# Where a gate's chunks of cached values stand in TensorE's order: between its halves, or all behind it

## The chip, the cores and the metric

One core of one Trainium2 chip runs the whole program. The metric is device time in microseconds (us) of one launch. Three runs of the kernel before gave 1912.76, 1916.53 and 1919.4 us; their median, 1916.53 us, is the time before. The profile was taken in a further execution of 1910.06 us.

## What is computed

Two decoder layers over 256 prompt tokens and 32 sample tokens (8 sequences of 4). Each layer projects the normed rows, mixes them by a pooling branch and by attention over three head groups, gates both branches, and adds a feed-forward part (dense in the first layer, experts in the second). The part around the change is the attention of the sample tokens over the caches, and the gates. Cut to that:

```python
u, q, k, v, gates = project(rmsnorm(xs, norm_attn[layer]), w_in[layer], ...)
for gi, (win, dil) in enumerate(ATT_GROUPS):        # (128,1), (512,4), (2048,16)
    c = caches[gi][layer]                            # keys c[:, :, 0], values c[:, :, 1]
    o, l = band_attention_sample(q[:, :, gi], k_all, v_all, n_past, dil, win // dil, slopes[gi])
...
g = sigmoid(gates)
h = g[..., 0, :] * (pool_o @ w_bp) + g[..., 1, :] * (att_o @ w_ba)
x = x + h @ w_o
```

All products with weights are done to float32 accuracy.

## The kernel before, in words

**Chunks.** Everything large comes from HBM in chunks of 1 MB, all issued by SyncE (SP) in one fixed order into a ring of five slots (RING, L54). Chunk c goes into the slot of chunk c-5, and SP waits in `send` (L819) until that one is done with: a weight chunk when VectorE (DVE) has made its low part (semaphore `lo_ready`), a cache chunk when TensorE (PE) has used it (`raw_used`). As SP waits in order, a chunk that can't be issued yet holds up all that stand behind it.

**Weights.** A weight chunk is split in two before PE uses it: `split_high` (L1544, ScalarE, ACT) and then `split_low` (L1824, DVE), into one of two split buffers. PE waits for the low part in `chunk` (L980). A tile of 128 output columns is 24 matmuls of 128x288.

**The stage of the change**, once per layer, stands between the scores over the cached keys and the branch tiles. On PE it has two kinds of work. Eight gates, G0 to G7, each one weight chunk of `w_in`, in two halves a and b of 24 matmuls (`gates`, L1272). And eighteen chunks of cached values, V0 to V17, four tiles each (`cache_values`, L1255): no split, PE multiplies the loaded chunk itself, with 32 columns of probabilities as weights. V0 and V9 open the sums of the first and the second four sequences and begin with three more matmuls for the new tokens. Behind G0b PE turns the probabilities of the second half (`turn_s_probs`), behind G4b it gathers the heads of the first four sequences (`gather_heads`, L1247), behind G7b those of the second. The order of both kinds is a table, `V_BEHIND` (L110): how many value chunks stand behind each half of each gate. `value_steps` (L113) makes PE's order of it (walked at L1278), `value_loads` (L127) makes SP's order.

A slot is told free late by a little: `release` (L1166) puts the signal on a list, and PE's next matmul that carries no signal of its own takes it along (`signal`, L944). The slot of a value chunk comes free when the first matmul behind the chunk is through.

**SP's order of the stage** is G0 V0 G1 V1 V2 G2 V3 V4 V5 G3 V6 V7 G4 V8 V9 V10 G5 V11 V12 G6 V13 V14 G7 V15 V16 V17, and then B0 to B3 (the branch weights, two loads of 512 KB each) and the four chunks of `w_out`. By the rule of five slots V3 takes the slot of V0, G3 that of V2, G4 that of V4, G5 that of V7, G6 that of V9, V13 that of V10, V17 that of V13, and B0 that of V14.

**The end of the stage.** DVE's list runs, for G7: the low part of B0 (`split_low`), then G7a's scaling, `own_columns(1)` (L2061) on the finished sum of the cached values, then G7b's scaling. PE's `gather_heads(1)` needs `own_columns(1)`, and so stands behind the splitting of B0. The branch tiles follow.

```python
for kind, n, x in V_STEPS:                 # L1278, PE
    if kind == "V":
        cache_values(n)
        continue
    gates(n, x)
```

Of the kernel before, what the change touches and what calls it, by code (L numbers as in the profile page):

```python
# [106 lines left out]
    return a.astype(np.float32), m.astype(np.float32), spread.astype(np.float32)  # L107


V_BEHIND = ((1, 1), (1, 1), (2, 1), (1, 1), (2, 1), (1, 1), (1, 1), (2, 0))  # L110


def value_steps():  # L113

    out, v = [], 0
    for gate, behind in enumerate(V_BEHIND):
        for x, n in enumerate(behind):
# [2452 lines left out]
```

How the kernel before makes its waits and increments, by code:

```python
            def wait_free(self, e, job):  # L706
                b, u = self.where[job]
                e.wait_ge(free[b], self.base(b) + u + 1)
# [1 line left out]
            def wait_full(self, e, job):  # L710
                b, u = self.where[job]
                e.wait_ge(full[b], self.base(b) + u + 1)
# [1 line left out]
            def wait_read(self, e, job):  # L714
                b, u = self.where[job]
                e.wait_ge(free[b], self.base(b) + u + 2)
# [1 line left out]
            def wait_before(self, e, bank):  # L719
                e.wait_ge(free[bank], self.base(bank) + self.start[bank] + 1)
# [26 lines left out]
        def wait_chunk(e, L, c):  # L748
            e.wait_ge(loaded[c % RING], 16 * (L * dmas_until(N_LAYER, c % RING) + dmas_until(c + 1, c % RING)))
# [1 line left out]
        def wait_expert_chunk(e, seq, c):  # L751
            e.wait_ge(expert_loaded[c % E_SEMS], 16 * (seq * (N_EXPERT // E_SEMS) + c // E_SEMS + 1))
# [5 lines left out]
        def wait_cache_slot(e, L, S, m):  # L758
            q = m // BH - CACHE_SLOTS // BH
            if q >= 0:
                half, n = q // NQ, q % NQ
                if n == NQ - 1:
                    S.wait_full(e, ("ss", half))
                else:
                    e.wait_ge(scored.sem, scored.at(L, half * (NQ - 1) + n + 1))
# [6 lines left out]
        def through_extras(e, item, at_end=None):  # L773
            e.wait_ge(flags_ready, 1)
            items = e.value_load(flags_i[0:1, 2, EXTRA - 1:EXTRA], min_val=NE, max_val=ITEMS)
            with e.If(items > NE):
                with e.Fori(0, EXTRA) as x:
```

## Time and profile before

| what | value |
| --- | --- |
| median of three runs | 1916.53 us (1912.76 to 1919.4) |
| the profiled execution, its span | 1910.06 us, 1908.1 us |
| PE busy | 1878.0 us (98%) |
| DVE, ACT, POOL busy | 637.6, 459.6, 194.1 us |
| granted TensorE clock, mean | 0.997 |
| DMA, whole span | 553.82 MB, mean 290 GB/s |
| 1 MB loads of cached keys and values | 72, median 5.6 us from issue to landing |

The profiled execution is 6.5 us under the median; 2 us of it lie around the span. Times in the rows are microseconds from the start of the span. PE is busy nearly everywhere, so the share of busy time says little; what counts for a stage is which wait ends last in it.

### The profile page before, as it was taken

To read this page: it belongs to the slowest core of one execution; us is meant where nothing else is said; L and a number is where in the kernel's file an instruction comes from. 1 tells how busy PE (TensorE), PEld (TensorE's weight loads), DVE (VectorE), ACT (ScalarE), POOL (GpSimd) and SP (SyncE) were. 2 spreads that over 40 slices of the span, in tenths; PEclk is the share of its full clock that TensorE was granted. 3 is DMA by queue.
4 is the path that set the end of the run, shared out by engine and by line. 5 is a ranking of instruction groups with operands and counts; after the bars stand their busy time and mean duration, and the time that the engine had idled before them with its cause. 6 is when DMAs were issued, how large, how long until landed. Compare 5 with 4: busy or idle time off the path is not lost.

```text
span 1908.1 us, 44773 instructions
## 1 busy us (share of the span) xinstructions
PE 1878.0 (98%) x20473; PEld 1281.4 (67%) x20474; DVE 637.6 (33%) x1074; ACT 459.6 (24%) x688; POOL 194.1 (10%) x264
## 2 busy tenths in 40 slices
PE   8999999999999999999999999999999999999998
PEld 8998877999999999877874453535445353444535
DVE  5556543754435466643541011110201011020101
ACT  5434442444334434443431000000000000000000
POOL 2114100233403113200100000000000000000000
PEclk9999999999999999999999999999999999999999
DMA  9444699645445445589547999999999999999996
GB/s 303 143 154 153 221 310 360 193 156 171 159 170 181 155 134 175 178 280 356 187 165 284 414 378 412 405 380 410 376 413 384 407 403 385 409 370 415 387 407 266
DMA packets 212399, 553.82 MB, mean 290 GB/s; under 512 B 11482, under 2 KB 107914, under 8 KB 195680
## 3 DMA queue, kind: packets, MB, share of 16 engines
q1 hardware_dynamic: 208864, 541.71, 76.7%
q0 software_dynamic: 3248, 9.18, 1.4%
q8 instruction: 164, 2.69, 0.6%
q14 instruction: 27, 0.22, 0.0%
q10 hardware_dynamic: 96, 0.02, 0.0%
HBM read 543.46 MB, written 7.77 MB: 289 GB/s over the span
## 4 chain that ended last, share of the span: by engine, by line
PE 94%; DVE 2%; ACT 1%; DMA 1%; issue 1%; POOL 0%; SPq 0%; DVEq 0%; ACTq 0%; POOLq 0%
PE psum L952 89%; PE psum L960 5%; DMA low_part<-in_w_branch_attn 1%; DVE w_split L1829 1%; ACT w_split L1550 0%; DVE low_part L1822 0%; DMA low_part<-in_x_sample 0%; DVE low_part L2326 0%; ACT low_part L1520 0%; DVE low_part L1941 0%; DVE high_part L1946 0%; DVE xn_split L1841 0%; DVE high_part L1866 0%; ACT low_part L1603 0%; SPq L814 0%
## 5 line engine op out<-in xcount | busy, mean ns | idle before, releaser
L952 PE MATMUL psum<-low_part 128*32 128x512 f32 (+3 forms) x6922 | 673.9, 526 | 0.9 <-DVE low_part L2218 0.9
L952 PEld LDWEIGHTS psum<-xn_split,w_split 128*128 128x128 f32 x3744 | 502.1, 188 | 36.6 <-issue 29.1
L952 PE MATMUL psum<-xn_split,w_split 128*128 128x288 f32 x3744 | 518.8, 297 | 1.4 <-DVE w_split L1829 1.3
L952 PEld LDWEIGHTS psum<-low_part 128*32 128x32 f32 (+2 forms) x6922 | 238.8, 114 | 391.8 <-issue 385.2
L952 PE MATMUL psum<-low_part,high_part 128*32 128x256 f32 (+3 forms) x6634 | 343.4, 360 | 4.6 <-DVE low_part L1822 2.3
L1829 DVE TENSOR_TENSOR w_split<-low_part,w_split 128x2048 fp32r<-128x2048 f32 x104 | 238.7, 2295 | 262.3 <-ACT w_split L1550 261.9
L952 PEld LDWEIGHTS psum<-low_part,high_part 128*32 128x32 f32 (+1 forms) x6634 | 216.9, 111 | 130.2 <-issue 15.7
L1550 ACT ACTIVATE w_split<-low_part 128x2048 fp32r<-128x2048 f32 x104 | 199.1, 1914 | 260.0 <-PE psum L952 215.9
L2338 DVE TENSOR_TENSOR low_part<-high_part,psum 128x384 f32<-128x384 f32 (+1 forms) x48 | 29.8, 621 | 426.2 <-PE psum L952 423.8
L960 PE MATMUL psum<-high_part,low_part 128*128 128x128 f32 (+2 forms) x839 | 110.1, 282 | 11.7 <-DMA low_part<-in_x_sample 7.4
L1793 ACT ACTIVATE high_part<-psum 128x384 f32<-128x384 f32 (+1 forms) x48 | 25.9, 544 | 395.0 <-PE psum L952 394.1
L1809 ACT ACTIVATE ye_split<-psum 128x256 fp32r<-128x256 f32 x24 | 7.5, 384 | 446.2 <-PE psum L952 446.2
L960 PEld LDWEIGHTS psum<-high_part,low_part 128*128 128x128 f32 (+2 forms) x839 | 92.9, 142 | 24.6 <-issue 14.6
L2314 DVE TENSOR_TENSOR ye_split<-psum,ye_split 128x256 fp32r<-128x256 f32 x24 | 8.7, 418 | 271.4 <-ACT ye_split L1809 271.4
L1520 ACT ACTIVATE low_part<-psum 128x512 f32<-128x512 f32 (+1 forms) x130 | 73.1, 592 | 103.6 <-PE psum L960 95.0
L1822 DVE COPY low_part<-psum 128x512 f32<-128x512 f32 (+6 forms) x108 | 63.4, 596 | 58.1 <-PE psum L960 55.9
L952 PE MATMUL psum<-hid_split,w_split 128*128 128x288 f32 x528 | 70.2, 295 | 0.7 <-DVE low_part L2160 0.7
L952 PEld LDWEIGHTS psum<-hid_split,w_split 128*128 128x128 f32 x528 | 70.0, 188 | 0.9 <-issue 0.9
L2326 DVE SCALAR_TENSOR_TENSOR low_part<-psum,low_part 128x256 f32<-128x256 f32 (+1 forms) x96 | 39.5, 473 | 70.5 <-PE psum L952 70.5
L952 PE MATMUL psum<-merged_high,w_split 128*128 128x288 f32 x256 | 53.3, 298 | 0.0
L2529 POOL TENSOR_TENSOR hid_split<-low_part,hid_split 128x288 fp32r<-128x288 f32 x22 | 36.9, 1698 | 77.6 <-ACT hid_split L1727 77.6
L952 PEld LDWEIGHTS psum<-merged_high,w_split 128*128 128x128 f32 x256 | 41.7, 188 | 3.0 <-issue 2.3
(162 smaller groups left out, 943.5 us busy)
## 6 DMA issues: line engine op xcount, KB each, us to landing
low_part<-in_we_down SPq DMA_DIRECT2D x112, 1024.0 KB, 8.4
low_part<-in_cache_kv_g SPq DMA_DIRECT2D x72, 1024.0 KB, 5.6
low_part<-in_we_gate SPq DMA_DIRECT2D x64, 1024.0 KB, 8.1
low_part<-in_we_up SPq DMA_DIRECT2D x64, 1024.0 KB, 8.4
low_part<-in_w_in SPq DMA_DIRECT2D x55, 1024.0 KB, 5.2
low_part<-in_we_gate SPq DMA_DIRECT2D x64, 768.0 KB, 7.8
low_part<-in_we_up SPq DMA_DIRECT2D x64, 768.0 KB, 6.9
low_part<-in_w_dense SPq DMA_DIRECT2D x33, 1024.0 KB, 5.3
```

The source lines that it names most:

```text
L952: signal(e.matmul(out, lhsT, rhs, start=start, stop=stop, skip_group_check=mixed), inc)
L960: signal(e.transpose(out, in_, ident[0:in_.shape[0], 0:in_.shape[0]]), inc)
L1520: S.freed(e.activation(out, in_, ACT.Copy), job)
L1550: e.activation(w_split[gw % SRING][:, 0, :], view(slot(c), CH), ACT.Copy).then_inc(hi_ready, 1)
L1793: I.freed(e.activation(m_sig[r][:, 0:EW[g]], I.ps(job)[:, 0:EW[g]], ACT.Silu), job)
L1809: e.activation(ye_split[:, 0, r, :], I.ps(("ed", r // 2))[:, 256 * (r % 2):256 * (r % 2 + 1)], ACT.Copy)\
L1822: S.freed(e.tensor_copy(out, in_), job)
L1829: e.tensor_tensor(s[:, 1, :], view(slot(c), CH), s[:, 0, :].bitcast(F32), ALU.subtract).then_inc(lo_ready, 1)
L2314: low = e.tensor_tensor(ye_split[:, 1, r, :], I.ps(job)[:, 256 * (r % 2):256 * (r % 2 + 1)], ye_split[:, 0, r, :].bitcast(F32), ALU.subtract)
L2326: I.freed(e.scalar_tensor_tensor(out=x, in0=I.ps(job)[0:n, 0:256], scalar=at_item(gate_of, tt, of)[0:n], in1=x, op0=ALU.mult, op1=ALU.add) ...
L2338: I.freed(e.tensor_tensor(m_h[r][:, 0:EW[g]], m_sig[r][:, 0:EW[g]], I.ps(job)[:, 0:EW[g]], ALU.mult), job)
L2529: e.tensor_tensor(hid_split[:, 1, f, :], hid[f % 4], hid_split[:, 0, f, :].bitcast(F32), ALU.subtract)\
```

## The change

One table changes. Before, each gate has one or two chunks of cached values behind its first half and one behind its second. After, both halves of G0 to G6 follow each other, and the two or three chunks stand behind the second. G7 is unchanged: two chunks between its halves.

```diff
-V_BEHIND = ((1, 1), (1, 1), (2, 1), (1, 1), (2, 1), (1, 1), (1, 1), (2, 0))
+V_BEHIND = ((0, 2), (0, 2), (0, 3), (0, 2), (0, 3), (0, 2), (0, 2), (2, 0))
```

The number of chunks per gate is the same. PE's order was

G0a V0 G0b V1 | G1a V2 G1b V3 | G2a V4 V5 G2b V6 | G3a V7 G3b V8 | G4a V9 V10 G4b V11 | G5a V12 G5b V13 | G6a V14 G6b V15 | G7a V16 V17 G7b

and becomes

G0a G0b V0 V1 | G1a G1b V2 V3 | G2a G2b V4 V5 V6 | G3a G3b V7 V8 | G4a G4b V9 V10 V11 | G5a G5b V12 V13 | G6a G6b V14 V15 | G7a V16 V17 G7b

SP's order comes out the same, chunk for chunk, and so do the slots. The programs of ACT, DVE and POOL don't change.

## Rows read from the trace of the kernel before

**Rows 1.** The page: the chain that ended last, by engine.

```profile
PE 94%; DVE 2%; ACT 1%; DMA 1%; issue 1%; POOL 0%; SPq 0%; DVEq 0%; ACTq 0%; POOLq 0%
```

**Rows 2.** Stage of both layers by windows: busy us, clock, DMA share, GB/s.

```profile
252.46:331.74 79.28, 78.85 (x559) 58.31 (x555) 30.06 (x34) 25.36 (x30) 0.00 (x0) 1.00 0.99 340
838.19:917.61 79.42, 78.84 (x559) 58.30 (x555) 30.07 (x34) 25.38 (x30) 0.00 (x0) 1.00 0.99 338
```

**Rows 3.** The chain, in order of time: start, length, what (first layer).

```profile
319.50 6.63 DMA low_part<-in_w_branch_attn
326.15 1.92 ACT w_split L1550
328.09 2.29 DVE w_split L1829
330.90 0.70 DVE low_part L2064
331.74 193.68 PE psum L952 x1450
```

**Rows 4.** PE's timeline in the stage, first layer: 128x288 a half, 128x512 value chunks.

```profile
259.62 3.46 PE L952 MATMUL psum<-xn_split,w_split 128*128 128x288 f32 x24
...
263.66 1.06 PE L952 MATMUL psum<-low_part 128*32 128x512 f32 x8
...
268.11 1.06 PE L952 MATMUL psum<-low_part 128*32 128x512 f32 x8
269.11 3.45 PE L952 MATMUL psum<-xn_split,w_split 128*128 128x288 f32 x24
272.49 1.06 PE L952 MATMUL psum<-low_part 128*32 128x512 f32 x8
...
276.87 1.92 PE L952 MATMUL psum<-low_part 128*32 128x512 f32 x16
278.73 3.46 PE L952 MATMUL psum<-xn_split,w_split 128*128 128x288 f32 x24
...
295.26 4.69 PE L952 MATMUL psum<-low_part 32*128 32x512 f32 x22
299.88 3.46 PE L952 MATMUL psum<-xn_split,w_split 128*128 128x288 f32 x24
...
304.07 1.07 PE L952 MATMUL psum<-low_part 128*32 128x512 f32 x8
```

**Rows 5.** PE's timeline in the input projection: two column tiles back to back.

```profile
53.88 6.64 PE L952 MATMUL psum<-xn_split,w_split 128*128 128x288 f32 x48
60.45 0.69 PE L952 MATMUL psum<-high_part 128*32 128x288 f32 x8
```

**Rows 6.** ACT's timeline: the splits of G3, G4, G5, G6 and B0, each waiting for its landing.

```profile
274.99 1.92 ACT L1550 ACTIVATE w_split<-low_part 128x2048 fp32r<-128x2048 f32 x1 [1.39 <-DMA low_part<-in_w_in]
285.14 1.91 ACT L1550 ACTIVATE w_split<-low_part 128x2048 fp32r<-128x2048 f32 x1 [0.86 <-DMA low_part<-in_w_in]
296.27 1.91 ACT L1550 ACTIVATE w_split<-low_part 128x2048 fp32r<-128x2048 f32 x1 [4.29 <-DMA low_part<-in_w_in]
305.13 1.92 ACT L1550 ACTIVATE w_split<-low_part 128x2048 fp32r<-128x2048 f32 x1 [0.76 <-DMA low_part<-in_w_in]
326.15 1.91 ACT L1550 ACTIVATE w_split<-low_part 128x2048 fp32r<-128x2048 f32 x1 [3.40 <-DMA low_part<-in_w_branch_attn]
```

**Rows 7.** SP's timeline and the DMA view of 299.96:299.98: G6's load, us to landing.

```profile
299.96 0.37 SPq L830 DMA_DIRECT2D low_part<-in_w_in  x1
...
low_part<-in_w_in SPq DMA_DIRECT2D x1, 1024.0 KB, 5.1
```

**Rows 8.** The lower clock in layer two: PE's timeline in both layers, window of 810.

```profile
225.99 1.97 PE L960 MATMUL psum<-high_part,low_part 128*128 128x128 f32 x16
...
806.45 4.32 PE L952 MATMUL psum<-low_part,high_part 128*128 128x32 f32 x56 [0.77 <-POOL high_part L796]
810.70 3.11 PE L960 MATMUL psum<-high_part,low_part 128*128 128x128 f32 x16
...
810.00:813.50 3.50, 3.50 (x31) 3.12 (x24) 0.69 (x1) 1.30 (x4) 0.00 (x0) 0.56 0.00 0
```

## The prediction

> **What bounds the kernel now.** I read the chain by engine first: it lies on TensorE (PE) for 94% [rows 1]. That invites the thought that fewer matmul changes are simply worth their time. So I looked at the stage of the change alone, by windows. It lasts 79.28 us in the first layer and 79.42 in the second; PE is busy for 78.85 and 78.84 of it, and the DMA engines for 0.99 of it, at 340 and 338 GB/s [rows 2]. Both are full. Which of them ends last is for the chain in order of time to say [rows 3]: at the stage's end it leaves PE and runs through the load of the branch weights, B0 (landed at 326.15), ScalarE's split (1.92), VectorE's (2.29), `own_columns` (0.70), and only then the matmuls of 331.74. From B0's landing to that matmul are 5.59 us. So the stage now ends when B0 lands, with PE waiting hardly at all: the two are level. I take the second layer as equal to the first, as its stage has the same length and the same busy times within 0.2 us [rows 2].
>
> **Prices on PE** [rows 4, 5]. A value chunk between two halves takes 1.00 us (268.11 to 269.11), two in a row 1.86 (276.87 to 278.73), so a further chunk 0.86. A half before a value chunk takes 3.38 (269.11 to 272.49). Two tiles of the same 24 matmuls back to back, with other work behind them, take 6.57 (53.88 to 60.45), against twice 3.38 = 6.76; the first of such a pair thus takes 3.19. Putting the halves together saves 0.19, the chunks together 0.14: 0.33 per gate, for seven gates 2.3 us a layer, 4.6 in all. Were PE alone the bound, that is the gain.
>
> **What the change does to the loads.** Nothing is added or taken away, and SP's order stays, but the moment at which a slot comes free moves. Every value chunk that stood between the halves now ends a half later, and SP is held at it, with all later loads behind. I follow this through the first layer by a few chunks.
>
> *V3* takes V0's slot, free once the matmul behind V0 is through. Now that is G0b, from 259.62. After the change it is V1, behind G0b, the turned probabilities and V0. V1 then ends at 259.62 + 4.04 (G0b and the turning, 259.62 to 263.66) + 0.86 - 0.19 = 264.33 [rows 4]. So V3 is issued at some 264.4, over 4 us later. A load into an idle queue takes 5.1 to 5.2 (G6 issued at 299.96, its split begun at 305.13) [rows 6, 7]: V3 lands at 269.6.
>
> *The rate of the stream* [rows 6]. From G3's landing (274.99) to G6's (305.13) ten chunks come in 30.14 us, and from G6's to B0's (326.15) seven in 21.02: 3.0 us each. The best stretch is G4 to G5, four in 11.13: 2.78. The worst is G3 to G4, three in 10.15: 3.38. I take 3.0, which both long stretches give.
>
> *G3 to G5.* G3 is the third behind V3: 278.6, against 274.99 now. G4 is three further, 287.6 (285.14 now); G5 four further, 299.6 (296.27 now). Loads are late by 2.5 to 3.6 us, the DMA queue having been idle for lack of a slot before V3.
>
> *V10.* Unhindered, PE would reach G4a at 264.33 + 3 x 6.57 + 1.86 + 2.72 + 1.86 = 290.5. But G4's split takes 1.92 + 2.29 from its landing, to 291.8, so G4a starts at 292.0. Now V9 and V10 stand between G4a and G4b; after the change G4b and the gathering come first, 4.19 us (299.88 to 304.07) [rows 4]. V10 ends at 292.0 + 3.19 + 4.19 + 4.62 (V9 and V10, 295.26 to 299.88) = 304.0. Now it ends at 299.88.
>
> *G6 to B0.* G6 takes V9's slot, which V10's matmuls release: issued at 304.1 in place of 299.96 [rows 7], landed at 309.3 (V12 has landed at 305.6, so here the queue runs dry again). Seven chunks of 3.0 later B0 lands at 330.3, against 326.15 now. The same seven from 305.13 give 326.1 for the kernel before, so the sum reproduces its own end. B0's own slot doesn't matter: V15, which releases it, ends near 322.3, early enough for 330.3.
>
> *The end.* The 5.59 us behind B0 are unchanged, so the branch tiles begin at 335.9, 4.2 late. PE finds G7 split at 322.6, does G7a, waits for V17 (327.3) and ends G7b near 331.7: it then stands idle for about 4 us where it now waits next to nothing. The saved 2.3 us are in that idle time.
>
> **Sum.** 4.2 us a layer. The matmuls from 331.74 run for 193.68 us of the chain without another step [rows 3], so nothing later takes the delay up. Twice 4.2 is 8.4: 1910.06 becomes 1918.5 for an execution like the profiled one; the median of the runs is 6.5 above it, and I put the forecast on the median, 1916.53 + 8.4 = 1924.9. ACT, DVE and POOL do the same work in the same order, and their busy times (25 and 30 of 79 us, POOL none) hide it [rows 2]; the gates' scaling gets later behind later splits, but the six banks hold the tiles until then.
>
> **Bounds.** At 2.78 per chunk throughout, G4 lands at 286.3 and its split is ready when PE is, V10 ends at 302.7, G6 lands at 307.9 and B0 at 327.4: 1.2 a layer, 2.4 in all. For the other end I let the worst stretch come again on loads that PE waits for: 10.15 in place of 9.0 for three chunks, once before G4 and once behind G6, adds 2.2 a layer: 6.4, or 12.8 in all. A gain at this step is excluded, unless chunks come faster than any row shows.
>
> **Rivals.**
>
> *The loads catch up.* With less idle DMA elsewhere, all chunks come at 2.78. For it: four in a row do. Against: both longer stretches average 3.0. It gives 1916.53 + 2.4 = 1918.9, within 0.3%, which is about what a measurement of this kernel can tell from no change.
>
> *The clock falls in the new idle time.* In the second layer, PE waited for POOL and then did narrow matmuls from 806.45; in the window behind it the granted clock is 0.56, near the lower level of 1.2 GHz, and 16 turnings took 3.11 us where the first layer's took 1.97 [rows 8]. The forecast makes an idle time of 4 us at each stage's end, longer than what the chain holds on other engines there now (0.70 and less once the split is done). One such fall costs at least 1.14, so two 2.3: 1924.9 + 2.3 = 1927.2. Against it: narrow work is not what stands before and behind this wait, halves and branch tiles are. The Trainium skill, "TensorE: Matmul & The Clock Gate", section "Why this matters for your kernels", asks for no idle gaps between bursts of matmuls, as the clock goes back to its lower level in them. By that rule this change would cost more than the sum; the trace bears it out in one place [rows 8], but shows no wait of this kind.
>
> *PE is the bound after all, and the kernel gets faster.* The place is the end of the stage: if B0 lands in time for a PE that is 2.3 us ahead, at 326.15 - 2.3 = 323.9, the gain of 4.6 stays and the time is 1911.9. G6 can't land before 307.9 (V10's end with no wait of PE, and 5.2), so seven chunks would have to come in 16.0 us, 2.29 each. That is the point from which it decides; the best of the rows is 2.78. For it speaks only that PE is busy throughout.
>
> **How the numbers follow.** The forecast has 0.54, the caught-up loads 0.24, the lower clock 0.16, the gain 0.06. Slower by over 0.3% (5.7 us) are the lower clock and nearly all of the forecast: 0.66. Within 0.3% are the caught-up loads and the forecast's lower edge: 0.28. Faster: 0.06. The range goes from just under the caught-up loads, 1916, to 1932, the upper bound of 12.8 with one to two falls of the clock; that leaves out the gain and the edges, under 2 in 10. Most of the chance lies on one sign, so one range will do.
>
> **What would show it.** In the changed kernel's stage: halves in pairs of 6.57, value runs of 1.86 and 2.72; V3's issue some 4 us later; G4's split begun near 287 to 288; V10's end and G6's issue 3 to 4 us later; B0's split begun near 330; PE idle for 3 to 4 us before `gather_heads(1)` and the DMA share of the stage below 0.99. Both stages should last 3 to 5 us longer, and everything else as long as now. I am wrong if B0 lands at 327 or sooner, if PE doesn't wait at the end, or if the delay is taken up behind the stage.

## The result, and the profile after

The changed kernel takes 1934.71 us (median of six, 1929.34 to 1935.43) against 1915.9 for the kernel before on the same chip: a ratio of 1.0094, interval 1.0077 to 1.0112, some 18 us slower. The sign was right; the time lies above the range of 1916 to 1932. The profiled execution has a span of 1932.7 us. It took 1935.43 us, 0.7 above its median, while the profiled execution of before took 1910.06, 5.8 under its own, so the two traces differ by more than the medians.

Both stages by windows, the stretches behind them, and five stretches inside (us, busy of PE, PEld, DVE, ACT, POOL, clock, DMA share, GB/s):

```profile
257.26:342.88 85.62, 77.03 (x559) 58.68 (x555) 30.14 (x34) 25.51 (x30) 0.00 (x0) 1.00 0.90 311
852.39:940.35 87.96, 80.03 (x559) 60.47 (x555) 30.15 (x34) 25.39 (x30) 0.00 (x0) 0.96 0.89 305
342.88:350.00 7.12, 7.12 (x34) 7.12 (x35) 3.77 (x4) 3.41 (x3) 0.00 (x0) 0.57 1.10 351
940.35:947.30 6.95, 6.95 (x33) 6.95 (x34) 3.60 (x4) 3.41 (x3) 0.00 (x0) 0.57 1.08 345
264.50:277.50 13.00, 13.00 (x87) 8.29 (x86) 3.98 (x5) 3.90 (x8) 0.00 (x0) 1.00 0.58 198
299.60:312.40 12.80, 12.80 (x90) 9.03 (x86) 4.70 (x5) 2.66 (x4) 0.00 (x0) 1.00 0.77 274
902.00:909.40 7.40, 7.40 (x34) 2.26 (x33) 3.12 (x3) 2.80 (x3) 0.00 (x0) 0.77 0.43 158
883.87:890.00 6.13, 6.13 (x35) 5.29 (x36) 0.85 (x3) 1.99 (x4) 0.00 (x0) 0.72 0.92 289
277.50:286.00 8.50, 8.50 (x68) 6.84 (x64) 0.00 (x0) 0.35 (x1) 0.00 (x0) 1.00 1.02 357
```

Against [rows 2] the stages are 6.3 and 8.5 us longer. PE's busy time in the first has fallen from 78.85 to 77.03: the pairing does save PE work. But the DMA engines, 0.99 busy over the stage before, now have two long pauses, ahead of V3 and ahead of G6: 0.58 and 0.77 in stretches where PE is busy throughout. The pause ahead of V3 was there before as well, but shorter. The same stretch of the kernel before, behind its G0a:

```profile
259.70:272.70 13.00, 12.97 (x98) 10.64 (x102) 3.76 (x5) 3.34 (x7) 0.00 (x0) 1.00 0.84 289
```

Behind each stage the granted clock is 0.57. In the second layer it also fell inside the stage (0.72 behind a wait for a value chunk, 0.77 at V9), and PE's busy time there is 3.0 us above that of the first.

The chain in order of time now leaves PE four times in the first layer's stage, where it left it once [rows 3]:

```profile
278.06 10.19 DMA low_part<-in_cache_kv_g
...
289.37 9.16 DMA low_part<-in_cache_kv_g
...
311.65 5.22 DMA low_part<-in_w_in
...
331.91 5.35 DMA low_part<-in_w_branch_attn
...
342.88 196.46 PE psum L952 x1450
```

PE's timeline in the first layer (idle time before an instruction in brackets, with what ended it):

```profile
284.16 1.92 PE L952 MATMUL psum<-low_part 128*32 128x512 f32 x16
288.30 1.06 PE L952 MATMUL psum<-low_part 128*32 128x512 f32 x8 [2.21 <-DMA low_part<-in_cache_kv_g]
...
298.57 1.07 PE L952 MATMUL psum<-low_part 128*32 128x512 f32 x8 [0.98 <-DMA low_part<-in_cache_kv_g]
...
306.95 5.55 PE L952 MATMUL psum<-low_part 32*128 32x512 f32 x30
...
322.63 6.62 PE L952 MATMUL psum<-xn_split,w_split 128*128 128x288 f32 x48 [1.69 <-DVE low_part L1822]
...
336.28 3.46 PE L952 MATMUL psum<-xn_split,w_split 128*128 128x288 f32 x24
342.88 1.86 PE L952 MATMUL psum<-high_part,low_part 128*128 128x16 f32 x8 [3.13 <-DVE low_part L2064]
344.57 5.42 PE L952 MATMUL psum<-pool_branch_split,w_split 128*128 128x288 f32 x24
```

V4 and V5 are through near 286.0, then PE waits for V6 to land. The waits at V8, G6a and at the stage's end follow. The last two lines run at the lower clock: the gathering and the first branch tile.

ACT's splits of G3 to G6 and B0, which answer to [rows 6]:

```profile
285.65 1.91 ACT L1550 ACTIVATE w_split<-low_part 128x2048 fp32r<-128x2048 f32 x1 [8.83 <-DMA low_part<-in_w_in]
...
293.86 1.92 ACT L1550 ACTIVATE w_split<-low_part 128x2048 fp32r<-128x2048 f32 x1 [1.41 <-DMA low_part<-in_w_in]
...
306.81 1.91 ACT L1550 ACTIVATE w_split<-low_part 128x2048 fp32r<-128x2048 f32 x1 [7.20 <-DMA low_part<-in_w_in]
...
316.90 1.92 ACT L1550 ACTIVATE w_split<-low_part 128x2048 fp32r<-128x2048 f32 x1 [4.35 <-DMA low_part<-in_w_in]
...
337.29 1.92 ACT L1550 ACTIVATE w_split<-low_part 128x2048 fp32r<-128x2048 f32 x1 [6.16 <-DMA low_part<-in_w_branch_attn]
```

From G0a's start (252.46 before, 257.26 after) these are:

| split begins | before | predicted | after |
| --- | --- | --- | --- |
| G3 | 22.5 | 26.1 | 28.4 |
| G4 | 32.7 | 35.1 | 36.6 |
| G5 | 43.8 | 47.1 | 49.6 |
| G6 | 52.7 | 56.8 | 59.6 |
| B0 | 73.7 | 77.8 | 80.0 |
| branch work begins | 79.3 | 83.4 | 85.6 |

SP's timeline, V3's, G3's and V8's issue:

```profile
269.20 0.37 SPq L830 DMA_DIRECT2D low_part<-in_cache_kv_g  x1
...
277.65 0.37 SPq L830 DMA_DIRECT2D low_part<-in_w_in  x1
...
289.37 0.37 SPq L830 DMA_DIRECT2D low_part<-in_cache_kv_g  x1
```

and the DMA view of G3's load alone (its last column: us from issue to landing):

```profile
low_part<-in_w_in SPq DMA_DIRECT2D x1, 1024.0 KB, 8.0
```

The stages and the slow stretches behind them make 6.3 + 8.5 + 2.8 + 2.7 = 20.3 us of the span's 24.6. The first stage also begins 4.8 us later, though the two programs are the same up to there: that goes with this one execution. All other stretches together are 0.5 shorter.

### The profile page after: what moved, and what is told of

It is laid out like the page before. It is cut to its first block, busy times and chain, and to the rows that moved or that the text cites. A ratio compares the mean times of both kernels' runs of the same rounds, so it can differ in the third digit from the quotient of the medians.

```text
span 1932.7 us, 44773 instructions
## 1 busy us (share of the span) xinstructions
PE 1886.7 (98%) x20473; PEld 1292.6 (67%) x20474; DVE 638.2 (33%) x1074; ACT 460.3 (24%) x688; POOL 194.2 (10%) x264
## 4 chain that ended last, share of the span: by engine, by line
PE 92%; DMA 3%; DVE 3%; ACT 1%; issue 1%; POOL 0%; DVEq 0%; SPq 0%; ACTq 0%; POOLq 0%
PE psum L952 87%; PE psum L960 5%; DMA low_part<-in_cache_kv_g 2%; DVE w_split L1829 1%; ACT w_split L1550 1%; DMA low_part<-in_w_branch_attn 1%; DMA low_part<-in_w_in 1%; DVE low_part L1822 0%; DMA low_part<-in_x_sample 0%; DVE low_part L2326 0%; ACT low_part L1520 0%; DVE xn_split L1841 0%; DVE low_part L1941 0%; DVE high_part L1946 0%; DVE high_part L1866 0%
## 5 line engine op out<-in xcount | busy, mean ns | idle before, releaser
L1822 DVE COPY low_part<-psum 128x512 f32<-128x512 f32 (+6 forms) x108 | 63.4, 596 | 62.9 <-PE psum L960 58.8
L2326 DVE SCALAR_TENSOR_TENSOR low_part<-psum,low_part 128x256 f32<-128x256 f32 (+1 forms) x96 | 39.5, 473 | 70.5 <-PE psum L952 70.5
```

The costliest lines, as they stand in the source:

```text
L1822: S.freed(e.tensor_copy(out, in_), job)
L2326: I.freed(e.scalar_tensor_tensor(out=x, in0=I.ps(job)[0:n, 0:256], scalar=at_item(gate_of, tt, of)[0:n], in1=x, op0=ALU.mult, op1=ALU.add) ...
```

## The experiments

Ratios are to the kernel before on the same chip, with 95% intervals; 0.001 is 1.9 us. The first theory was that the loss is the late handing back of slots, and with it the loads; part of it the clock. Against it stood: something else in the paired order, an even cost per gate, or the runs of chunks as such.

**e1 and e2: quarter loads.** Each value chunk loads one of its four sequences; the products over the other three use what the slot held. Keys and weights are loaded whole.

```diff
-send(L, c, [(view(slot(c), BH, 512), src)])
+held = BH if kv == 0 else 1
+send(L, c, [(view(slot(c), BH, 512)[:, 0:held], src[:, 0:held])])
```

The order of before (e1):

> The order of before, but each chunk of cached values loads only a quarter of itself (one of its four sequences, 256 KB); the other three quarters are what the slot held. PE's work is unchanged. Theory 1 (loads set the stage's end): before is level between loads and PE, so taking three quarters of the value loads away gives back only the 0.4 to 0.5 us of PE's waiting per layer: before minus 0 to 2 us. Theory 2 (PE's own order or the engines' waits set the time): the same. This run is the base for the next.

The changed order (e2):

> The changed order with the same quarter loads. Theory 1 (late loads are the whole loss): no load is late any more, PE stands idle nowhere in the stage, the clock stays up, and the pairing's saving of 0.33 us per gate shows: 3 to 5 us faster than the order of before with the same loads, both stages near 77 us. Theory 2 (something else in the order, as the gates' evictions or the splits behind paired halves, costs the 19 us): as slow as the changed kernel, over 10 us slower than the order of before with these loads.

e1: 0.9986 (0.9965 to 1.0006), which takes in the expected 0 to 2 us. e2: 1.0019 (1.0004 to 1.0033), so 6 us slower than e1 (some 1.5 to 11 by the two intervals): not the gain of theory 1, and theory 2's 10 us only at the edge. The stage by windows, of e1:

```profile
256.06:334.78 78.72, 78.68 (x558) 58.35 (x555) 29.92 (x33) 25.28 (x30) 0.00 (x0) 1.00 0.55 180
```

and of e2, second layer:

```profile
845.72:925.96 80.24, 76.63 (x558) 58.90 (x555) 30.14 (x34) 25.28 (x30) 0.00 (x0) 1.00 0.52 170
```

PE's work falls by 78.68 - 76.63 = 2.05 us (predicted 2.3), and yet the stage is longer, with the DMA engines half idle. So the loss doesn't need full DMA engines. PE's timeline of e2, first layer, shows where:

```profile
317.75 6.62 PE L953 MATMUL psum<-xn_split,w_split 128*128 128x288 f32 x48 [0.92 <-DVE low_part L1823]
...
337.64 1.04 PE L953 MATMUL psum<-high_part,low_part 128*128 128x16 f32 x8 [2.78 <-DVE low_part L2065]
```

B0 is waited for: a slot freed late, then a load's own time, then both splits, is too long a way even with half the DMA time free. The wait ahead of G6a ends with a copy of DVE that frees its bank, and that copy stands behind G6's split (see e13). In the second layer the two waits come to 3.5 us, more than the 2.05 saved.

**e3: own signal.** In the changed kernel a chunk tells its slot free with its own last matmul (V8 and V17 excepted, whose last matmul has another signal to carry). Cut from the edit:

```diff
-   full[S.bank(job)] if last else None, mixed=True)
-release(n)
+ends = last or TILES[n + 1][0] != TILES[n][0]
...
+   full[S.bank(job)] if last else raw_used if ends else None, mixed=True)
+if last:
+    release(n)
```

> The changed order with full loads, but a chunk of cached values tells its slot free with its own last matmul, where it now rides on the next matmul, which in a run of chunks waits for the next chunk's landing. Theory A (the riding signal ties each load to the landing of the chunk behind: V5's slot, used up at 286.0, is told free only when V6 has landed at 288.3, and so on): 2 to 4 us per layer come back, 4 to 8 in all, and V8 is issued within 0.5 us of the end of V5's matmuls. Theory B (it is the later place of the chunks alone): 0 to 2 us come back.

1.0057 (1.0033 to 1.0081): some 7 us back, and by the two intervals 1 to 13. That a gain is there is shown, barely; its size is not. The traces decide for theory A. PE's timeline:

```profile
279.80 1.92 PE L952 MATMUL psum<-low_part 128*32 128x512 f32 x16
283.20 1.06 PE L952 MATMUL psum<-low_part 128*32 128x512 f32 x8 [1.47 <-DMA low_part<-in_cache_kv_g]
```

and SP's, V8:

```profile
281.79 0.71 SPq L830 DMA_DIRECT2D low_part<-in_cache_kv_g  x1
```

V5 ends near 281.7 and V8 goes out at 281.79, ahead of V6's start at 283.20. In the changed kernel it went out at 289.37, a microsecond behind V6's start and 3.4 behind the end of V5. The order alone did not do this: a signal that rides on the next matmul waits with it. The rest of the stage follows, ACT's splits of G6 and B0 and both stages by windows:

```profile
309.62 1.92 ACT L1553 ACTIVATE w_split<-low_part 128x2048 fp32r<-128x2048 f32 x1 [3.50 <-DMA low_part<-in_w_in]
...
330.31 1.92 ACT L1553 ACTIVATE w_split<-low_part 128x2048 fp32r<-128x2048 f32 x1 [6.20 <-DMA low_part<-in_w_branch_attn]
```

```profile
252.91:335.89 82.98, 77.03 (x558) 58.66 (x555) 30.14 (x34) 25.37 (x30) 0.00 (x0) 1.00 0.94 323
843.96:926.59 82.63, 76.84 (x558) 58.78 (x555) 30.14 (x34) 25.37 (x30) 0.00 (x0) 1.00 0.93 323
```

Behind G0a's start G6 is split at 56.7 and B0 at 77.4, where the prediction had 56.8 and 77.8 and the changed kernel 59.6 and 80.0.

**e4: the wait filled.** Six matmuls without use, ahead of the last gathering.

```diff
 S.wait_free(e, job)
+for _ in range(6 if half == 1 else 0):
+    mm(S.ps(job)[:, 0:T], ident, xT[:, 0, :], True, True)
 S.wait_read(e, ("OS", half))
```

> The changed kernel with six idle matmuls (128x288, float32, into the bank that the last gathering then overwrites) ahead of gather_heads(1) in each layer, some 3 us of work in a wait of 3.1 to 4.0 us. Theory 1 (PE's idle time at the stage's end lets the clock fall to its lower level, and the gathering and the first branch tile then take 6.95 us where they took 4.16): the granted clock stays 1.00 behind the stage, 2 to 2.8 us per layer come back, 4 to 5.6 in all. Theory 2 (the clock falls there for another reason): no gain, or slower by the matmuls.

1.0046 (1.0021 to 1.0071): some 9 us back, by the two intervals 3 to 15, so the middle is above the 4 to 5.6 expected and the interval takes them in. Behind the first layer's stage, by windows:

```profile
342.00:349.10 7.10, 7.10 (x54) 7.10 (x55) 4.63 (x6) 3.42 (x3) 0.00 (x0) 1.00 1.10 349
```

and PE's timeline:

```profile
342.00 1.06 PE L952 MATMUL psum<-high_part,low_part 128*128 128x16 f32 x8 [0.40 <-DVE low_part L2066]
342.92 3.45 PE L952 MATMUL psum<-pool_branch_split,w_split 128*128 128x288 f32 x24
```

The clock stays at 1.00, and the gathering and first tile take 0.92 and 3.45 in place of 1.69 and 5.42: 2.74 us per layer. The stages are 85.5 and 85.1 us long, the first as in the changed kernel, the second without its falls of the clock at 883.87 and 902.00. Over all runs: behind the eight stages whose wait was filled (e4, e9, e12, e14) the clock is 1.00 over the next 7 us; behind the seven with an unfilled wait of 3.1 to 4.0 us (the changed kernel, e3, e8, e13) it is 0.51 to 0.64. So the fall behind the stage is a matter of the idle wait: shown.

**e5, e6, e8: which gate.** Only G0 paired; only G6; all but G6.

```diff
-V_BEHIND = ((1, 1), (1, 1), (2, 1), (1, 1), (2, 1), (1, 1), (1, 1), (2, 0))
+V_BEHIND = ((0, 2), (1, 1), (2, 1), (1, 1), (2, 1), (1, 1), (1, 1), (2, 0))   # e5
+V_BEHIND = ((1, 1), (1, 1), (2, 1), (1, 1), (2, 1), (1, 1), (0, 2), (2, 0))   # e6
+V_BEHIND = ((0, 2), (0, 2), (0, 3), (0, 2), (0, 3), (0, 2), (1, 1), (2, 0))   # e8
```

> Only G0 is paired (its V0 and V1 behind G0b), all other gates as before. Theory 1 (each pairing hands slots back late, and what counts is whether a later wait ends later for it): V3 is issued some 4.3 us later as in the changed kernel, G3's split begins 26 us into the stage instead of 22.5, which PE can still meet at G3a (30.3), and the loads behind are fed by slots that come free as before; so B0 lands within 1 us of before: 0 to 2 us slower in all, no fall of the clock at the stage's end. Theory 2 (an early delay of the queue is never made up, as loads and PE are level): B0 lands 2 to 4 us later in each layer, 6 to 12 us slower in all with the clock's fall.

> Only G6 is paired (V14 and V15 behind G6b). Theory 1: V14 hands its slot to B0 at some 70 us into the stage instead of 66.2; with 6.2 us from there to B0's landing it lands at 76 instead of 73.7, PE waits some 2.5 to 3 us ahead of gather_heads(1), and the clock may fall there: 2.4 us per layer from the landing and up to 2.8 from the clock, 5 to 10 us slower in all, more than half of it in this one gate. Theory 2 (the loss is spread evenly over the seven gates): 19 us over seven, 2 to 3 us slower.

> G0 to G5 paired, G6 with one chunk behind each half as before. Theory 1 as I hold it: V14's slot was not what held B0 in the changed kernel (it landed 2.7 us behind V17, in the stream), so the stream from G6's late landing still sets the end: B0 lands 78 to 80 us into the stage, and 12 to 18 us of the loss stay. Theory 2 (the last gate's late slot is what costs): under 8 us of the loss stay.

e5: 0.9997 (0.9985 to 1.0008), nothing lost that can be measured, though V3 goes out late. e6: 1.0036 (1.0025 to 1.0047), 7 us from one gate. e8: 1.0069 (1.0050 to 1.0088), 13 us stay; theory 1 in all three. G6 alone costs 7 and the others without it 13; all together cost 18, which these intervals can't tell from the sum of 20 (the table further down can). The traces show that B0's landing is the later of two: in e8 it comes 3.0 us behind V17 in the stream, as in the changed kernel (2.7); in e6 it is issued only as V17 lands, held by its own slot. PE's timeline of e6, first layer, and the window behind the second layer's stage:

```profile
334.56 1.03 PE L952 MATMUL psum<-high_part,low_part 128*128 128x16 f32 x8 [2.76 <-DVE low_part L2064]
```

```profile
926.20:933.00 6.80, 6.80 (x41) 6.80 (x42) 4.27 (x5) 3.41 (x3) 0.00 (x0) 0.75 1.10 348
```

**e12: e6 with its wait filled** (five matmuls, as in e4).

> G6 alone paired, with five idle matmuls (some 2.4 us) in the wait ahead of gather_heads(1). Theory 1: the pairing of G6 alone cost 7 us, of which the later landing of B0 makes 2 to 2.5 us per layer (4 to 5 in all) and the clock behind the idle time the rest; with the wait filled 2 to 3 us come back, and 4 to 5 us over before stay. Rival (the clock is not part of it in this kernel): all 7 us stay, or more.

1.0003 (0.9990 to 1.0017): some 6 us come back, more than expected. The stages are 80.9 and 80.8 us long, 1.5 longer than before; the 3 us that this makes lie at the interval's edge. That the clock was the larger part for one paired gate does not follow: see the table further down.

**e7: the runs between the halves.**

```diff
+V_BEHIND = ((2, 0), (2, 0), (3, 0), (2, 0), (3, 0), (2, 0), (2, 0), (2, 0))
```

> The runs of two or three chunks all stand between the halves: (2,0), (2,0), (3,0), (2,0), (3,0), (2,0), (2,0), (2,0). PE's pairing of halves stays (the second half and the next gate's first), but each chunk ends no later than before, and the second of each gate a half earlier. Theory 1 (what cost was the later release): slots come free up to a half earlier, no load is issued later than before, B0's slot comes free at G6b's start as before or sooner, and the saving of PE (0.33 us per gate, 4.6 in all) is free as far as the loads can follow: 0 to 4 us faster than before, the end still set by B0's landing. Theory 2 (runs of chunks cost by themselves, as their loads have to be in at once): slower than before, with waits of PE at the second chunk of the runs.

1.0035 (1.0021 to 1.0048): theory 1 failed here. Slots came free earlier, but chunks were also wanted earlier than they land, PE's timeline:

```profile
280.96 1.07 PE L952 MATMUL psum<-low_part 128*32 128x512 f32 x8 [0.68 <-DMA low_part<-in_cache_kv_g]
...
291.36 1.07 PE L952 MATMUL psum<-low_part 128*32 128x512 f32 x8 [1.75 <-DMA low_part<-in_cache_kv_g]
```

These waits make 2.4 us of the 5.4 that PE waits in this stage. Another 2.0 are waits for banks that ACT (L1716, ahead of G1a) and DVE (L1822, ahead of G6a) free, and 0.9 stand at the end. So e7 is in part, not wholly, theory 2: a run asks for its chunks at once and hands their slots back at once, and in this ring of five both groupings lost. No run varied the number of slots.

**e9, e13, e14: how far the edits go together.** e9 has e3's and e4's edits. e13 has another, alone: DVE copies the first gathered heads ahead of G6's split.

```diff
 if n == EX0_GATE:
     own_columns(0)
+elif n == EX0_GATE + 1:
+    sample_out(0)
```

> The changed order with both edits: a value chunk tells its slot free with its own last matmul, and six idle matmuls stand ahead of gather_heads(1). Alone they gave back 7 (1.0094 to 1.0057) and 9 us (1.0094 to 1.0046). Theory A (two costs beside each other: the riding signal, and the clock at the stage's end): the gains add, some 2 to 4 us over before are left, and both stages are 82 to 83 us long with the granted clock 1.00 behind them. Theory B (one cost seen twice): 7 us or more over before are left.

> The changed kernel, but VectorE copies the gathered heads of the first four sequences (sample_out(0)) ahead of G6's split, not behind it and G5's two scalings, so that G6a's bank is free when G6 is split. Theory 1 (the bank adds some 1.4 us to G6a's start, and V13's slot, told free by G6a's first matmul, passes it on to V17 and B0): G6a begins within 0.3 us of the end of G6's split, B0 lands 0 to 1.5 us sooner, 0 to 3 us of the 18 come back. Theory 2 (the stream of loads sets B0, whenever G6a begins): less than 1 us comes back.

> The changed order with all three edits: own signal, early sample_out(0), six idle matmuls. Theory 1: of the 6.5 us that the two left, 1 to 3 come back; both stages are 81 to 83 us long, as the loads behind V3, V8 and G6 are still issued late, and 3 to 5 us over before are left. Theory 2 (the three edits take away everything that the order costs): within 2 us of before or faster.

e9: 1.0034 (1.0020 to 1.0049), 6.5 us left, between the theories. That the gains overlap in part is what the middles say (7 and 9 alone, 11.5 together); the intervals leave it open. e13: 1.0067 (1.0043 to 1.0091); its interval overlaps that of the changed kernel, so its gain is not shown. What its trace shows is the wait itself. Of the changed kernel, DVE's timeline:

```profile
318.85 2.29 DVE L1829 TENSOR_TENSOR w_split<-low_part,w_split 128x2048 fp32r<-128x2048 f32 x1 [6.83 <-ACT w_split L1550]
321.06 1.05 DVE L2108 TENSOR_TENSOR low_part<-psum,low_part 128x288 f32<-128x288 f32 x2
322.26 0.23 DVE L1822 COPY low_part<-psum 128x64 f32<-128x64 f32 x1
```

G6's split ends at 321.1, but G6a began at 322.63: its bank holds the gathered heads, which DVE copies out behind the split and G5's scalings. In e13 the split ends at 317.70 and G6a begins 0.12 later, PE's timeline (the view ends at 320):

```profile
317.82 2.39 PE L952 MATMUL psum<-xn_split,w_split 128*128 128x288 f32 x16
```

e14, all three edits: 1.0022 (1.0008 to 1.0036), 4 us left, as theory 1 had it. Its first stage:

```profile
255.84:338.80 82.96, 79.77 (x570) 60.70 (x566) 30.04 (x34) 25.38 (x30) 0.00 (x0) 1.00 0.94 322
```

82.96 us against 79.28. What is left of waits in it is 2.2 us for a value chunk and 1.0 at the end. That both come of the loads' later place is argued: no run took that away alone.

**e10, e11: the other way.** The own signal in the kernel before, and with G0 paired as well, the try for a version that beats both.

> The order of before, with the own signal. Theory A: single chunks between halves never wait on the signal's carrier, which is a matmul of a gate whose weights are there, so a slot comes free 0.3 to 0.9 us sooner and no more; B0's load is issued that much sooner and the 0.4 to 0.5 us of waiting at the stage's end go: 0 to 2 us faster. Theory B (the carried signal is a cost of the stage in any order): 4 us or more faster.

> G0 alone paired, with the own signal: the try for a version that beats both. Theory 1: pairing G0 costs nothing (0.9997) because a later V3 is made up; with the slot told free sooner its two waits (0.5 to 1.0 us) go and PE's 0.33 us per layer show: 0 to 3 us faster than before. Rival: the loads are level with PE, and nothing is left to gain: within 2 us of before.

e10: 1.0000 (0.9985 to 1.0015). e11: 0.9992 (0.9981 to 1.0002). With single chunks the riding signal costs nothing that can be measured, and e11's gain is not shown. No version was found that is faster than the kernel before beyond the interval.

**How much of it is the clock.** Every execution has a mean granted clock on record. In 28 executions of the kernel before, those beside e9 to e12, the span ran from 1907.2 us (clock 0.998) to 1921.7 (0.990), and span times clock is 1902.8 on average, with a standard deviation of 1.2, where that of the spans is 3.1. So most of the scatter is clock, and span times clock compares two kernels as if both ran at full clock. What the span has above it went to the clock (an upper estimate: idle time at the lower clock is counted in, though it costs nothing). Means in us, less those of the kernel before on the same chip:

| kernel | at full clock | to the clock |
| --- | --- | --- |
| changed | 9.3 to 10.1 | 6.7 to 8.7 |
| e3, own signal | 7.1 | 2.2 |
| e4, filled | 9.8 | -1.1 |
| e9, both | 8.0 | -1.5 |
| e14, all three | 6.6 | -1.5 |
| e1, quarter loads before | -1.6 | -2.3 |
| e2, quarter loads after | 2.3 | 1.2 |
| e5, G0 alone | 1.2 | -0.3 |
| e6, G6 alone | 3.7 | 3.2 |
| e12, the same, filled | 3.9 | -2.9 |
| e8, all but G6 | 10.5 | 6.1 |
| e7, between the halves | 6.5 | -0.7 |

For the changed kernel the clocks of before are not on record in the same batch; its row takes the four batches that are. So of its 18 us some 10 are waits and some 8 the clock. The filling gives back the clock's part alone; the own signal gives back some 2 to 3 us of waits and, with them, falls of the clock. The waits of e6 and e8, 3.7 and 10.5, don't add to those of all gates together. And e12 keeps the waits of e6: it comes out level with the kernel before only because the clock took less from it.

## Why the prediction was wrong

**What held.** The two are level, the loads end last: held; the chain now goes through them four times. PE's saving: 1.82 us measured in the first layer and 2.05 in e2, 2.3 predicted, and lost in idle time as said. V3's late issue: predicted 11.9 us behind G0a's start, measured 11.94 (269.20), and G3's load, which was the next to hang on it, went out at 20.4, where the same working puts it. The last seven chunks, G6 to B0: predicted 21.0, measured 20.4. The way from B0 to the branch work: 5.59, as before. The sum had 8.4 us for all this; the profile has 20.3. Two steps make up the difference.

**The first step that failed is the stream** ("G3 is the third behind V3: 278.6"; "G4 is three further"). It let chunks follow each other at 3.0 us from V3's landing to V12's, as if each were issued in time. V6, the second behind V5, landed 7.8 us after it (280.4 to 288.25) in place of 6.0, and held PE for 2.21 us. The DMA engines did not stand still there (1.02 at 357 GB/s from 277.50 to 286.00), so why V6 was so late is open. Its wait fed back by the riding signal: V5's slot was told free only with V6's matmuls, so V8 went out at 32.1 in place of some 29, landed late and held PE again. G4a began at 299.57, 42.3 behind G0a and not 39.5 (292.0), and G6, B0 and the branch work followed. I had described that signal ahead of the prediction and let it ride in the sum, but always on a matmul that doesn't wait. B0 missed its forecast by 2.2 us in the first layer; G3 had missed by 2.3, G4 by 1.5, G6 by 2.8 (table above). In e3, where a chunk tells its slot free itself, the working comes out: G6 at 56.7 and B0 at 77.4, within 0.4 of the forecast, though e3 also sends V3 0.8 us sooner, so the agreement is in part luck. In all, this step makes some 3.4 of the missing 11.9 us: 2.1 in the first layer, and in the second 4.3 less the 3.0 by which PE was busy longer at the lower clock.

**The second and larger step is the clock, for which the sum had nothing.** It was a rival at 0.16, and it came true together with the forecast. The clock fell behind both stages. I had argued that narrow work was not at hand there; the idle wait of 3.1 and 4.0 us sufficed. Its price was 2.74 per layer by e4's rows, where I had put at least 1.14 from another stretch. In the second layer it fell inside the stage as well, 3.0 us of PE's time. Together 8.5 us in this profile, and some 8 by the means of all executions. By the rule of the Trainium skill, "TensorE: Matmul & The Clock Gate", section "Why this matters for your kernels", such waits were to be feared, and the trace agrees: 0.57 behind the wait, 1.00 once it is filled. Of five waits of 1.9 to 2.8 us at the stage's end (e2, e3, e6), three had the fall behind them and two had not. A forecast of a long idle wait should have carried the fall in its sum.

**A wait that the sum had wrong.** "The six banks hold the tiles until then" fails at G6a, whose bank is DVE's to free behind the split: 1.5 us at that place. What it adds to the whole stays open: e13's gain is not shown.

**The range** took the worst stretch twice, 6.4 us a layer (twice 1.15 is 2.3 and not 2.2, but nothing hangs on it). That covered the first layer's 6.3, not the second's 8.5. It added one to two falls of the clock at 1.14 each, where the two behind the stages cost 5.5 and those inside the second stage came on top.

## What to carry to other kernels

When two resources are level, grouping work on one of them moves the moments at which buffers come back; follow every buffer's return through its load and what stands between load and use, and look for the place where the ring runs dry, not only at the mean rate. A release that rides on the next instruction is free while that instruction never waits, and ties one load to the next as soon as it does. Idle time that a change makes on TensorE can cost twice: once itself (here 3.1 and 4.0 us) and once in the slower clock behind it (2.74).

## What was not expected of the hardware

The clock also fell inside the second layer's stage, with PE busy for all of 7.40 us (902.00 to 909.40, clock 0.77): at V9, whose first matmuls have only 32 rows. The same piece of work took 7.25 us there and 5.55 at 306.95 in the first layer. The order of before has such falls too. In e10 they stand in the second layer's stage behind the beginnings of V0 and V9, with PE busy throughout, by windows:

```profile
846.60:850.00 3.40, 3.40 (x15) 1.58 (x15) 0.80 (x2) 0.44 (x1) 0.00 (x0) 0.50 0.36 88
887.55:890.95 3.40, 3.40 (x17) 0.59 (x16) 2.07 (x1) 1.30 (x1) 0.00 (x0) 0.50 0.50 171
```

That stage is 3.5 us longer than e10's first (82.2 against 78.7). In e6, with the same two falls, it is 2.3 (83.6 against 81.3), although its wait at the end is the shorter one. The profile of before has none in either stage. So both orders can have them. There is one profile per kernel; that they come and go between executions is argued from the mean clocks above.

A load of 1 MB with nothing or almost nothing ahead of it landed 5.1 to 5.3 us after its issue (V3 and G6 in the changed kernel's two layers), and every 2.6 to 3.0 us in most of a stream. Of three loads issued within a microsecond the first took 8.0 us (G3) and 9.2 (V8), but that is no fixed price: in e4, with the same order and signals up to there, G3 took 5.2, and V6 behind it 10.3 (10.2 in the changed kernel). What came late in both was the pair, V6 7.8 and 8.6 us behind V5.
